# Two-layer block on one core: rows of three norms' roots brought to all partitions by DMA through device memory

## What is computed

```python
def rms_norm(x, g):
    xf = x.astype(jnp.float32)
    y = xf * lax.rsqrt(jnp.mean(xf * xf, axis=-1, keepdims=True) + EPS)
    return (y * g.astype(jnp.float32)).astype(x.dtype)

# first block
h = rms_norm(x, norm_g)
proj = jnp.einsum('bsd,de->bse', h, w_in)
(fq, fk, fv, fg, ff, px, pg, sq, sk, sv, sg) = jnp.split(proj, idx, axis=-1)
# two attentions and a pool over these, gated; x = x + mixed @ w_out

# second block
h = rmsnorm(x, mix_pre_norm[i])
z = h @ w_in[i]          # latents lq, lkv for an attention; b, c, xv for a short convolution
...
h = rmsnorm(x, ffn_pre_norm[i])
f = (jax.nn.silu(h @ w_gate[i]) * (h @ w_up[i])) @ w_down[i]
x = x + rmsnorm(f, ffn_post_norm[i])
e = rmsnorm(p[i] @ w_ple_proj[i], ple_norm[i])
x = x + jax.nn.sigmoid(x @ w_ple_gate[i]) * e
```

## Time and profile before

| | |
|---|---|
| median of 3 runs | 897.88 us |
| profiled execution | 898.78 us |
| its span, first to last instruction | 897.1 us |
| TensorE busy | 890.1 us, 99% |
| VectorE busy | 398.9 us, 44% |
| ScalarE busy | 342.9 us, 38% |
| GpSimd busy | 497.5 us, 55% |
| device memory read, written | 80.93 MB, 2.10 MB |
| granted TensorE clock | 1.0 in the whole span |

### The profile page before, as it was taken

One profiled execution on the slowest core, in us unless ns is written; L12 is line 12 of the kernel. 1 busy time (PEld: TensorE's weight loads), 2 busy tenths in 40 slices (PEclk: granted clock), 3 DMA queues, 4 the chain that ended last, 5 costly groups with the idle time before them and its releaser, 6 DMA issues.

```text
span 897.1 us, 12872 instructions
## 1 busy us (share of the span) xinstructions
PE 890.1 (99%) x4488; PEld 731.7 (82%) x4488; DVE 398.9 (44%) x690; ACT 342.9 (38%) x693; POOL 497.5 (55%) x515
## 2 busy tenths in 40 slices
PE   8999999999999999999999999999999999999998
PEld 7889887777779888876779888888888888888887
DVE  2663495777742743865667611111111112223672
ACT  4333403567715130566648532222222223223421
POOL 6988885321475877923336554444444455555453
PEclk9999999999999999999999999999999999999999
DMA  6332363212222422221012332223322322233213
GB/s 213 125 124 89 117 167 100 64 48 96 72 73 73 137 95 80 109 71 47 25 48 94 113 123 94 94 96 100 106 95 94 117 94 94 94 98 101 73 58 117
DMA packets 29468, 85.77 MB, mean 96 GB/s; under 512 B 5193, under 2 KB 8161, under 8 KB 29425
## 3 DMA queue, kind: packets, MB, share of 16 engines
q1 hardware_dynamic: 24528, 78.65, 26.6%
q10 hardware_dynamic: 4896, 6.53, 2.6%
HBM read 80.93 MB, written 2.10 MB: 93 GB/s over the span
## 4 chain that ended last, share of the span: by engine, by line
PE 96%; DMA 1%; POOL 1%; DVE 1%; ACT 0%; SPq 0%; issue 0%; DVEq 0%; ACTq 0%
PE bank L505 28%; PE bank L507 28%; PE bank L506 28%; PE bank L562 5%; PE bank L750 2%; PE bank L1089 2%; PE bank L853 1%; DMA raw<-in_weights 1%; POOL w_lo L458 1%; PE bank L845 1%; PE bank L882 1%; PE bank L817 0%; PE bank L814 0%; PE bank L729 0%; SPq L378 0%
## 5 line engine op out<-in xcount | busy, mean ns | idle before, releaser
L458 POOL TENSOR_TENSOR w_lo<-raw,w_hi 128x256 fp32r<-128x256 f32 (+1 forms) x420 | 409.6, 1003 | 205.7 <-ACT w_hi L1334 199.8
L505 PE MATMUL bank<-aT_hi,w_hi 128*128 128x512 f32 (+1 forms) x584 | 225.8, 387 | 0.0
L507 PE MATMUL bank<-aT_hi,w_lo 128*128 128x512 f32 (+1 forms) x584 | 222.4, 381 | 0.0
L506 PE MATMUL bank<-aT_lo,w_hi 128*128 128x512 f32 (+1 forms) x584 | 222.2, 380 | 0.0
L505 PE MATMUL bank<-w_hi,aT_hi 128*128 128x512 f32 (+3 forms) x576 | 218.5, 379 | 1.0 <-POOL w_lo L438 0.6
L507 PE MATMUL bank<-w_hi,aT_lo 128*128 128x512 f32 (+3 forms) x576 | 213.1, 370 | 0.0
L506 PE MATMUL bank<-w_lo,aT_hi 128*128 128x512 f32 (+3 forms) x576 | 212.9, 370 | 0.0
L450 POOL TENSOR_SCALAR w_hi<-raw 128x1024 fp32r<-128x1024 f32 x70 | 77.4, 1105 | 172.7 <-PE bank L507 142.3
L1334 ACT ACTIVATE w_hi<-raw 128x1024 fp32r<-128x1024 f32 x70 | 74.1, 1060 | 231.3 <-PE bank L507 215.7
L507 PEld LDWEIGHTS bank<-aT_hi,w_lo 128*128 128x128 f32 x584 | 109.8, 188 | 21.2
L506 PEld LDWEIGHTS bank<-aT_lo,w_hi 128*128 128x128 f32 x584 | 110.0, 188 | 19.8 <-issue 0.2
(11 more groups left out here) (228 smaller groups left out, 892.0 us busy)
## 6 DMA issues: line engine op xcount, KB each, us to landing
raw<-in_weights SPq DMA_DIRECT2D x141, 512.0 KB, 3.3
x<-in_x ACTq DMA_DIRECT2D x4, 512.0 KB, 5.3
y_out<-x SPq DMA_DIRECT2D x7, 256.0 KB, 4.1
x<-in_x SPq DMA_DIRECT2D x3, 512.0 KB, 8.7
g_post<-in_gains ACTq DMA_DIRECT2D x3, 512.0 KB, 3.4
k_twice<-k_twice ACTq DMA_DIRECT2D x2, 512.0 KB, 5.6
x<-in_x SPq DMA_DIRECT2D x2, 256.0 KB, 4.0
raw<-in_weights SPq DMA_DIRECT2D x2, 256.0 KB, 4.2
```

What stands on the lines that cost most here:

```text
L458: lo = nc.gpsimd.tensor_tensor(w_lo[:, s, at], raw[:, r, at], w_hi[:, s, at].bitcast(F32), ALU.subtract)
L505: mm(out, st_hi, mv_hi, start=start, stop=False)
L506: mm(out, st_hi, mv_lo, start=False, stop=False)
L507: return mm(out, st_lo, mv_hi, start=False, stop=stop)
```

## The change

TensorE's turns of the broadcast columns go, with their banks and waits, and VectorE's copies. In their place ScalarE issues two transfers for each of the three norms. `roots_to_row` stores the column of four on 128 partitions as a row of 512 words in a small tensor in device memory, `r_rows`: 512 words that lie singly in the tensor's order. `row_to_all` waits on ScalarE until that transfer has landed and then loads the row to all 128 partitions of `R`. VectorE waits on `R_in` in place of its copy.

```diff
+        r_rows = nc.dram_tensor("r_rows", (3, S), F32).ap()
...
-            pe.wait_ge(r_made, 1)
-            bank_free(("R1", 0))
-            for t in range(T):
-                last = turn(tbank(("R1", 0))[:, t * P:(t + 1) * P], stat[:, 3, t:t + 1].broadcast_to([P, P]))
-            last.then_inc(tile_full, 1)
...
+            def roots_to_row(n, of):
+
+                act_.dma_start(r_rows[n, :].rearrange("(t p) -> p t", p=P), of, allow_slow_non_contiguous=True)\
+                    .then_inc(r_row_out, 16)
+
+            def row_to_all(n):
+
+                act_.wait_ge(r_row_out, n * 16 + 16)
+                act_.dma_start(R[:, :], r_rows[n:n + 1, :].broadcast_to([P, S])).then_inc(R_in, 16)
...
             act_.wait_ge(r_made, 1)
+            roots_to_row(0, stat[:, 3, 0:T])
             qk_rows("fq", 0)
+            row_to_all(0)
             act_.dma_start(g_post[:, :], gains_d[3, :, :]).then_inc(g_post_in, 16)
...
             act_.wait_ge(r_made, 2)
+            roots_to_row(1, stat[:, 2, 4:4 + T])
             for name, dst, w, at0 in (("lq", lat_q, LQ_W, 48), ("lkv", lat_kv, RANK, 52)):
+                if name == "lkv":
+                    row_to_all(1)
...
             for t in range(T):
                 squares(emb[:, t, :], 40 + t)
+                if t == 0:
+                    act_.wait_ge(r_made, 3)
+                    roots_to_row(2, stat[:, 3, 12:12 + T])
+                elif t == 2:
+                    row_to_all(2)
             rsqrt(slice(40, 44))
...
             heads_lo("qT", q_parts, q_parts, col("gq"), q_hi, q_lo)
-            full(dve, ("R1", 0))
-            drain(("R1", 0), V.tensor_copy(R[:, :], tbank(("R1", 0))[:, :]))
-            dve.wait_ge(drained["dve"], order[0])
+            dve.wait_ge(R_in, 16)
             qk_norm(T)
```

More of the change, by code:

```diff
@@ L97, in psum_tiles @@
     group("fk", (0, 1, 2, 3), "act", ("fk", 3))
-    tiles["R1", 0] = (7, "dve", None)
     group("sf", (4, 5, 6, 7), "act", ("sf", 2))
@@ L123, in psum_tiles @@
     group("lkv", (5, 6, 7, 2), "act", ("lkv", 1))
-    tiles["R2", 0] = (3, "dve", None)
     n = 0
@@ L158, in psum_tiles @@
                 tiles["h3", t // 2, j] = (4 + j, "dve", None)
-    tiles["R3", 0] = (4, "dve", None)
     for t in range(T):
@@ L319, in hybrid_kernel @@
         masks_made, ident_made = sem("masks_made"), sem("ident_made")
-        w_half, r_made, R_made = sem("w_half"), sem("r_made"), sem("R_made")
+        w_half, r_made = sem("w_half"), sem("r_made")
+        r_row_out, R_in = sem("r_row_out"), sem("R_in")
         gate_scaled, gate_made = sem("gate_scaled"), sem("gate_made")
@@ L985, in _ @@
                            [(CH["lkv"], (0, 1, 2, 3)), (CH["lkv"] + 1, (4, 5, 6, 7))], RANK)
[L986 to L990, removed]
             def turn_lats():
@@ L1154, in ffn_first @@
                 for b in range(3):
[L1155 to L1161, removed]
                     ffn_part(b, slice(S // 2, S), b == 0).then_inc(w_used, 1)
@@ L2195, in _ @@
             V.sem_inc(roped, 1)
-            full(dve, ("R2", 0))
-            drain(("R2", 0), V.tensor_copy(R[:, :], tbank(("R2", 0))[:, :]))
-            dve.wait_ge(drained["dve"], order[0])
+            dve.wait_ge(R_in, 32)
             own(V.memset(u[:, :, 0:KERNEL - 1], 0.0))
@@ L2348, in _ @@
             rsqrt(slice(40, 44), D)
-            full(dve, ("R3", 0))
-            drain(("R3", 0), V.tensor_copy(R[:, :], tbank(("R3", 0))[:, :]))
-            dve.wait_ge(drained["dve"], order[0])
+            dve.wait_ge(R_in, 48)
             def emb_row(t):
```

## The result

The changed kernel is slower: 912.55 us median (910.37 to 914.69) against 897.91 us before on the same chip, ratio 1.0157, 95% interval 1.0146 to 1.0168. On a second chip it was 911.71 against 898.21 us, 1.0146 (1.0132 to 1.0159). The forecast was 896.6 us, in a range of 895.8 to 897.9.

A forecast was written before the change was run, and what follows sets the result against it. TensorE's queue was taken as the bound, busy 890.1 of 897.1 us. Removing the turns saved 1.3 us and the added transfers cost nothing at all three places: 897.88 - 1.3 = 896.6 us, range 895.8 to 897.9.

The forecast's parts named there:

- The turns, 1.3 us off TensorE: Twelve broadcast-column turns leave TensorE's queue, three sets of 0.44 us; 1.3 us saved, bounds 1.26 and 1.32.
- The landing of the scattered store: ScalarE's store of 512 single words at each norm lands after 3.2 us, bounds 1.9 and 4.5.
- The broadcast: Load of the row to 128 partitions takes 2.7 us; at the third place over 4 us before TensorE feels it.
- First place, cost nothing: At the fq norm, 13.8 us of cover before TensorE needs its product, against 5.3 us of ScalarE delay at most.
- Second place, cost nothing: Between lq activations and first lkv tile, ScalarE's idle time takes the wait and issue; `R` needed 18 us later.
- the hole: ScalarE's 6.09 us idle before the first lkv tile, expected to take up to 4.5 us wait and 0.33 us issue.
- Third place, cost nothing: Before the second feed-forward block, ScalarE's work runs 1.15 us late, with 1.0 us of cover left for TensorE.
- rival 2: Slower: ScalarE blocked at the third place, TensorE idle before its second feed-forward block; 900.4 us at 8 us landing; chance 0.06.
- No gain: Whole kernel: the saved time returns as TensorE's wait on weights; 897.9 us, chance 0.05.
- the faster rival: TensorE's queue pays each turn's whole duration, 12 x 0.272 = 3.3 us saved; 894.6 us, milder form 896.0; chance 0.08.

The follow-up runs named there:

- rows16_again: Changed kernel with each store as 128 pieces of 16 bytes at all three places, measured again with more rounds; 897.29 against 898.21 us before, 0.9993.
- the second place alone: Kernel before with only the second norm's root spread by transfers, turns kept at the other two; 897.73 against 898.04 us, 0.9996.
- store1_alone: Kernel before with all its turns, plus a 512-word store at the first place that nobody waits for or reads; 902.42 us, 1.0042.
- p1_late: Only the first norm by transfers, ScalarE's wait and broadcast moved behind the two loads and root that follow; 904.34 us, 1.0065 against kernel before.
- p3_late: Only the third norm by transfers, ScalarE's wait and broadcast moved behind the next chunk's high part; 904.56 us, 1.007 against kernel before.
- store1_half: Kernel before with its turns, plus an unread store of 256 single words at the first place; 903.66 us, 1.0059.

## Why the prediction was wrong

- **The turns, 1.3 us off TensorE: not refuted.** Twelve instructions fewer, 1.5 us less busy in `rows16_again`, and 1.05 and 0.92 us less time where nothing else stops TensorE; 0.31 for the second place alone, where 0.44 was the term, within its interval.
- **The landing of the scattered store: the step that failed.** Taken 3.2 us between bounds of 1.9 and 4.5; measured 8.8, 11.6 and 12.0. The nearest row was taken to be `g_col`, 1,024 scattered words that are read, and pos_i, read too, gave the upper bound. The prediction noted that the trace had no write of single words and kept the bound all the same. Reads of words say nothing of writes: 1,024 read in 2.8 to 3.8 us, 512 written next to each other in 8.5 to 12.2.
- **The broadcast: mis-sized.** Taken 2.7, at most 3.3; measured 4.4 to 5.2, and 3.0 to 4.9 behind the stores of 16 bytes. That it had over 4 us of cover was wrong even for the early landing. Between `R` and TensorE stand a product, a silu and a gated product, 2.2 us in the changed kernel (516.44 to 518.60); with `R` at 503.0 they would have ended at 505.2, about 2 us ahead of 507.24.
- **First place, cost nothing: wrong, by a path that was not in the working.** Cover was counted for ScalarE's queue and for `R`, and TensorE indeed did not wait for either. The working left out who else uses the DMA engines meanwhile: SyncE's next weight load, 2.1 us behind the store in another queue. `store1_alone` shows it without any wait on ScalarE. The rest of the wait (5.8 us in place of 3.4) came with a low half of 4.67 us in place of 2.77, beside the product that ScalarE's wait had delayed. In time this share is not shown: `p1_late` takes the product out of the way, and with a later landing TensorE waited 4.8 us all the same.
- **Second place, cost nothing: right.** The wait outgrew the hole (ScalarE stood 6.88 us in place of 6.09) and the weight load was late as well, but `R` was not needed for another 13 us and TensorE never waited.
- **Third place, cost nothing: wrong; rival 2's place and sign, but another path binds.** Its formula, stall equals landing less 501.3, gives for 8.82 us 497.13 + 8.82 - 501.3 = 4.65 us, near the 5.1 measured. But `p3_late` takes ScalarE's blockade away and keeps the stop. What binds is `R`, which the working had dismissed; in the changed kernel the path through ScalarE would have ended about 1 us sooner. Rival 2 was given 0.06 because no small transfer of the earlier trace rows came near 7.3 us; every one of those rows is a load, but for the 128 KB store. Its sentence from the Trainium skill ("DMA: Bandwidth & Descriptors", Anatomy of one DMA, which describes transfers that GpSimd issues: the receipt, slow with device memory as the target) pointed to the right side; yet the target alone is not it, since the same words 64 bytes apart land there in 1.8 us.
- **The clock: missing in every sum.** Each stop of 4.5 us and more was followed by a stretch at 0.5; in the changed kernel's profile that cost 1.4 and 1.9 us more. Rival 2's 900.4 us, with a stall of 3.8 us, carries nothing for it.
- **No gain, and the faster rival:** neither happened.

## What to carry to other kernels

A small transfer was priced here by its direction, its target and how its pieces lie there, not by its bytes; where the trace has no write like it, the bound from reads is no bound. When a change adds transfers, look in the trace for every load that is issued in the next ten microseconds on any queue, and ask who waits for it. If a column must go to device memory as a row, let each partition write its values as one piece and permute on the reading side, where it cost 0.4 us of VectorE for each product and nothing of the path.

## What the runs showed of the hardware that was not expected

- Single words written side by side to device memory: 8.5 to 12.2 us until they land, for 128, 256 or 512 of them; at 8 bytes' distance 4.9 us, at 64 bytes' 1.8 us; pieces of 16 bytes side by side 1.4 to 4.4 us.
- While they are under way, a load from device memory on another queue moves almost nothing: 0.07 MB from 26 to 34 us in place of 0.80, and its first 16 packets took 4.9 us each in place of 0.17.
- Spreading a row of 2 KB from one partition of the chip to the other 127 took 13.6 and 13.95 us, at most two packets at a time; from device memory to 128 partitions it took 3.0 to 5.8 us. Source and number of rows differ, and which of them counts is open.
- VectorE's product with a tile read at a step of four words took 1.09 us in place of 0.69.
- A wait of 3.4 us of TensorE (`store1_alone`) left the granted clock at 1.00, one of 3.7 us at the same place (`store1_half`) was followed by 0.67 over 46 to 50 us.
